# Two transformer blocks on one core: a load, two low parts, a window step and a value product in another order, and banks opened one by one

## The reference

```python
mod = (silu(c) @ w_ada + b_ada)                 # six vectors of 1024: "ada" panels of 512 columns
h = rms_norm(x, norm1_w) * (1 + scale1) + shift1
gq, gk, gv, gz, ga, gb, sq, sk, sv = split(h @ w_in)
beta = sigmoid(gb); g = -exp(a_log) * softplus(ga + dt_bias)     # gates, one row per head
o_g = gated_delta_rule_chunked(l2(gq), l2(gk), gv, g, beta)      # chunks of 64
o_s = sliding_window_attention(rms(sq), rms(sk), sv, sinks)
x = x + gate1 * (concat(o_g, o_s) @ w_out)
x = x + gate2 * ((silu(h2 @ w_gate) * (h2 @ w_up)) @ w_down)
# second block: conformer gate "cu", latent attention over 8 heads, gates "gl"
```

## Time and profile before

| | us |
|---|---|
| median of 3 runs | 1240.29 |
| lowest, highest | 1240.02, 1241.54 |
| the profiled execution | 1240.17 |
| its span, first to last instruction | 1238.1 |
| granted TensorE clock | 1.000 in the mean |
| PE busy | 1211.9 (98%) |
| DVE busy | 707.2 (57%) |
| ACT busy | 505.1 (41%) |
| POOL busy | 107.8 (9%) |
| HBM | 124 MB, 100 GB/s over the span |

### The profile page before, as it was taken

The page is one execution under the profiler, slowest core; times in us unless marked ns, Lnnn a source line. Parts: engine busy times, 40 slices in busy tenths (PEclk is TensorE's granted clock), DMA queues, the critical chain, the costliest instruction groups (busy, mean ns, idle before and its releaser), DMA issues.

```text
span 1238.1 us, 19976 instructions
## 1 busy us (share of the span) xinstructions
PE 1211.9 (98%) x8398; PEld 995.2 (80%) x8398; DVE 707.2 (57%) x1036; ACT 505.1 (41%) x795; POOL 107.8 (9%) x152
## 2 busy tenths in 40 slices
PE   6999999999999999999999999999999999999998
PEld 4788778789888888888888889898876778888886
DVE  5899979645485543323233567768765554433344
ACT  4475543663346222222223353225465663222232
POOL 4000006520020000000000110000012310000000
PEclk9999999999999999999999999999999999999999
DMA  9665711003023552243322342234123025333301
GB/s 339 217 213 193 245 35 38 3 4 105 20 86 101 170 162 77 77 128 102 102 77 64 107 138 77 94 94 86 48 69 81 1 73 140 89 91 105 106 35 68
DMA packets 149928, 125.58 MB, mean 101 GB/s; under 512 B 15952, under 2 KB 133489, under 8 KB 149712
## 3 DMA queue, kind: packets, MB, share of 16 engines
q1 hardware_dynamic: 148416, 121.98, 32.5%
q0 software_dynamic: 1232, 2.07, 0.5%
q10 hardware_dynamic: 192, 0.27, 0.1%
HBM read 122.20 MB, written 2.10 MB: 100 GB/s over the span
## 4 chain that ended last, share of the span: by engine, by line
PE 87%; DVE 8%; ACT 2%; issue 1%; DMA 1%; DVEq 0%; POOL 0%; ACTq 0%
PE bank L614 50%; PE bank L921 6%; PE bank L721 4%; PE bank L1397 4%; PE bank L1367 4%; PE bank L1431 4%; PE bank L754 2%; DVE post L2235 2%; PE bank L1286 2%; PE bank L1113 1%; DVE wlo L2201 1%; DVE arena L2353 1%; PE bank L672 1%; PE bank L1322 1%; PE bank L1339 1%
## 5 line engine op out<-in xcount | busy, mean ns | idle before, releaser
L614 PE MATMUL bank<-hsplit,whi 128*128 128x512 f32 (+1 forms) x1840 | 540.5, 378 | 4.1 <-DVE wlo L2201 4.1
L614 PEld LDWEIGHTS bank<-hsplit,whi 128*128 128x128 f32 x1840 | 335.2, 188 | 72.2 <-issue 7.8
L614 PE MATMUL bank<-hsplit,wlo 128*128 128x512 f32 (+1 forms) x920 | 346.0, 376 | 0.0
L2201 DVE TENSOR_TENSOR wlo<-ring,whi 128x2048 fp32r<-128x2048 f32 (+4 forms) x100 | 200.4, 2005 | 178.3 <-ACT whi L1636 178.0
L1636 ACT ACTIVATE whi<-ring 128x2048 fp32r<-128x2048 f32 (+4 forms) x100 | 168.6, 1686 | 125.5 <-DVE xT L2615 53.3
L614 PEld LDWEIGHTS bank<-hsplit,wlo 128*128 128x128 f32 x920 | 172.9, 188 | 32.4
L614 PE MATMUL bank<-a_split,whi 128*128 128x512 f32 x340 | 104.6, 389 | 0.0
L614 PEld LDWEIGHTS bank<-a_split,whi 128*128 128x128 f32 x340 | 63.8, 188 | 13.3
L614 PE MATMUL bank<-a_split,wlo 128*128 128x512 f32 x170 | 66.1, 389 | 0.0
L1579 POOL TENSOR_TENSOR acc<-acc,tb 128x512 f32<-128x512 f32 x12 | 17.8, 1479 | 423.1 <-ACT tb L1904 423.1
L1640 ACT ACTIVATE a_split<-tb 128x512 fp32r<-128x512 f32 x22 | 13.8, 632 | 88.0 <-DVE tb L2665 87.9
(11 more groups left out here) (491 smaller groups left out, 1803.8 us busy)
## 6 DMA issues: line engine op xcount, KB each, us to landing
ring<-in_w_in_dram SPq DMA_DIRECT2D x22, 1024.0 KB, 5.3
ring<-in_w_in_dram SPq DMA_DIRECT2D x34, 512.0 KB, 5.2
ring<-in_w_ada_dram SPq DMA_DIRECT2D x16, 1024.0 KB, 5.2
ring<-in_w_gate_dram SPq DMA_DIRECT2D x11, 1024.0 KB, 5.4
ring<-in_w_up_dram SPq DMA_DIRECT2D x11, 1024.0 KB, 5.3
ring<-in_w_down_dram SPq DMA_DIRECT2D x8, 768.0 KB, 4.8
ring<-in_w_down_dram SPq DMA_DIRECT2D x8, 640.0 KB, 4.4
hscratch<-in_w_ada_dram SPq DMA_DIRECT2D x4, 1024.0 KB, 14.9
```

The source lines that it names most:

```text
L614: last = mm(o[0:m, 0:n], w[:, k, c0:c0 + m], rhs(s, k), start=k + i == 0, stop=k == kn - 1 and i == 2)
L2201: split_lo = splitter(dve, None, lambda lo, src, hi: tt(lo, src, hi, ALU.subtract))
```

## The change

Eight edits, all of order:

- the first half of the eighth ada panel is now followed by sq0, the second half by sq1; ada 9 comes behind as before
- on DVE, `ada_sum(8)` is called in halves, with the `split_lo` that writes sq0's low part between them
- the `split_lo` of gz0 moves from behind `row_parts(1, ...)` to ahead of the wait for `egb`, that is ahead of the 8-row reciprocal
- in the first gz tile `gate_cols` moves from behind k step 5 to behind k step 7
- of the four window steps beside the `p2` gathers on DVE the last one moves ahead of its gather
- the `split_lo` of out3 moves from behind `raw_rest` of m = 3 to just behind `residual` of m = 3
- `first_tiles` opens each tile's bank just before the tile's first matmul
- `ml_values(29)` moves from the end of the attention's loop to behind k step 1 of the first late gl tile, ahead of `ml_turn(30)`

```diff
+        def ada_half_panel(i, h):
+            panel(f"ada{i}{h}", 4, 512, [(0, 512, w_cols(w_ada, 512 * i, 512, 4 * h, 4))], split=False)
+
         def ada_panel(i):
             for h in range(2):
-                panel(f"ada{i}{h}", 4, 512, [(0, 512, w_cols(w_ada, 512 * i, 512, 4 * h, 4))], split=False)
+                ada_half_panel(i, h)
...
         cols_panel("sv", w_in, 2704, 128)
         ada_panel(7)
-        ada_panel(8)
         for i in range(2):
+            ada_half_panel(8, i)
             cols_panel(f"sq{i}", w_in, 2064 + 256 * i)
         ada_panel(9)
...
             def first_tiles(name, chunk_ready, parts, order=range(KD), between={}):
-                outs = [open_tile(pe, *part[0]) for part in parts]
+                outs = []
                 pe.wait_ge(*done("w_lo", name))
                 hi, lo = split_of(name)
                 for at, k in enumerate(order):
                     pe.wait_ge(*chunk_ready(k))
-                    for o, (key, c0, n, rhs) in zip(outs, parts):
+                    for x, (key, c0, n, rhs) in enumerate(parts):
+                        if at == 0:
+                            outs.append(open_tile(pe, *key))
+                        o = outs[x]
...
-            amid_gz = [{1: [(ada, 9)], 3: [(query_lengths, 3)], 5: [(gate_cols,)], 7: [(gate_rows, 0)]},
+            amid_gz = [{1: [(ada, 9)], 3: [(query_lengths, 3)], 7: [(gate_cols,), (gate_rows, 0)]},
                        {3: [(gate_rows, 1)]}, {1: [(gate_rows, 2)], 7: [(gate_rows, 3)]}, {}]
...
-                if u >= 2 and u % 2:
+                if u >= 2 and u % 2 and u < len(MLU) - 1:
                     ml_values(u - 2)
-            amid_gl = {1: [(ml_turn, len(MLU) - 2)], 4: [(ml_turn, len(MLU) - 1)], 7: [(ml_values, len(MLU) - 1)]}
+            amid_gl = {1: [(ml_values, len(MLU) - 3), (ml_turn, len(MLU) - 2)], 4: [(ml_turn, len(MLU) - 1)], 7: [(ml_values, len(MLU) - 1)]}
...
             ada_mod(6)
-            ada_sum(8)
+            ada_sum(8, 0)
             split_lo()
+            ada_sum(8, 1)
...
             link(row_parts(0, grow, HD, HD + 32, 0))
+            split_lo()
             dve.wait_ge(*done("act_vectors", "egb"))
             link(ts(gate_tmp[0][32:40, :], gate_tmp[0][32:40, :], 1.0, None, ALU.add))
             link(v.reciprocal(gate_tmp[0][32:40, :], gate_tmp[0][32:40, :]))
             link(v.tensor_copy(grow[64:72, :], gate_tmp[0][32:40, :]))
             link(tt(glog[32:40, :], gate_tmp[0][32:40, :], grow[32:40, :], ALU.mult))
             link(row_parts(1, glog, 32, 0, 32))
-            split_lo()
...
             for j in range(NJ):
+                if j == NJ - 1:
+                    window(3 * NJ + 1 + j)
                 dve.wait_ge(*copied("p1", j))
                 gather("p2", j)
-                window(3 * NJ + 1 + j)
+                if j < NJ - 1:
+                    window(3 * NJ + 1 + j)
...
             for m in range(KD):
                 residual(("mo", m), m, 16)
-                if m == 0:
+                if m in (0, 3):
                     split_lo()
...
                 raw_rest("2", m, modA2[:, m:m + 1])
-                if m == 3:
-                    split_lo()
```

## The result

The changed kernel takes **1234.26 us** in the median of six runs (1232.18 to 1234.98), and the kernel before, run beside it, 1241.59 (1240.02 to 1242.36): a ratio of 0.9941, 95% interval 0.9931 to 0.9951. Forecast were 1232.7; the forecast alone spans 1231.8 to 1234, and down to its first two rivals it reaches 1236.4. The measured median lies 0.3 above the first of these ends and inside the second. The profiled execution took 1234.98 us for a span of 1233.2, so it lies above the median; why is the main finding of this study.

A forecast was written before the change was run, and what follows sets the result against it. TensorE (PE) was taken as the bound, busy 1211.9 of 1238.1 us, so only its idle time could be won. Six gains summed to 7.6 us: 1240.17 - 7.6 + 0.12 = 1232.7 us, range 1231.8 to 1234, to 1236.4 with rivals 1 and 2.

The forecast's parts named there:

- sq0, 2.2: First sq0 matmul: earlier load and low part between the `ada_sum(8)` halves start it at about 130.6; gain 2.2 us.
- gz0, 1.4: First gz0 matmul: low part written ahead of the 8-row reciprocal, so PE no longer waits; gain 1.4 us, lower bound 0.9.
- rival 1: DVE becomes the bound between 133 and 168 us, both first gains lost at `gate_cols`: 1236.3 us; chance 0.12.
- Window: Window step ahead of the last gather: POOL's product comes earlier and PE starts at 255.45; gain 0.95 us.
- out3: out3's low part behind `residual` 3 ends at 347.2, PE wants it at 349.0; gain 0.85 us, not under 0.6.
- By starts, not by shown ends: Stalls counted from matmul starts rather than estimated ends: sum about 7.7 us instead of 7.0.
- Banks: `cu` panel: banks opened singly let matmuls begin in two free banks during ACT's copies; gain 1.1 us, 0.3 to 1.2.
- values: `ml_values(29)`: two k steps of gl now lie between turn 29 and its values; gain 1.1 us, lower bound 0.8.
- rival 2: The small gains don't come (single waits cost as much as the common one, POOL hinders): 1235.3 us; chance 0.08.
- It adds and removes no instruction; all is order: Premise for the whole change: the edits only reorder existing work, and its parts are then priced one by one.
- Margin 0.3 us: At `gate_cols` behind k = 7: the scan it needs ends at 164.4, PE gets there at 164.8.
- if PE's busy time grew by what its idle time lost: Sign that the prediction is wrong; PE's busy time was expected to stay at 1212 us.

The follow-up runs named there:

- e7: Kernel before with only the new load order (no halves of `ada_sum(8)`), the window step and the single banks: 1241.20 us, ratio 1.0002.
- e8: Kernel before with `ada_sum(8)` halves (old load order), gz0's low part earlier (`gate_cols` left at k = 5), out3 and value products: 1239.20 us, ratio 0.9985.
- e2: Changed kernel with `gate_cols` put back behind k step 5, the other seven edits kept: 1233.81 us, ratio 0.9943.
- e1: Changed kernel run again with nothing edited: 1234.04 us, ratio 0.9946.
- e3: Changed kernel with `gate_rows(0)` moved on behind k step 1 of the second gz tile: 1232.10 us, ratio 0.9929.
- e5: Changed kernel, small groups still side by side, bank waits removed by moving DVE's ada 8 and 9 sums and ACT's gz 0 copy earlier: 1232.43 us, ratio 0.9930.
- e9: Kernel before run again unchanged, for a profile: 1241.48 us at a clock of 0.997.
- e6: Version of e3 with ScalarE's Ln and its table load moved behind the copy and square of the first sq tile: 1231.89 us, ratio 0.9926.
- e10: Version of e6 with the old load order of sq0 and `ada_sum(8)` in one piece: 1236.93 us, ratio 0.9965.
- e4: Kernel before with one edit alone, `gate_cols` moved behind k step 7, right ahead of `gate_rows(0)`: 1242.49 us, ratio 1.0014.
- run 24: Not a label but a count: 24 of 45 runs of the unchanged kernel before show a clock of 0.997 or less, median 1241.9 us.

## Why the prediction was right, and where it was not

The forecast of 1232.7 lies 1.6 us below the measured median, which is inside its range down to the rivals; its six terms come to 7.6 us where the trace shows 7.85. The six gains came as the mechanism had it. Step by step, with the steps of the table:

- **sq0, 2.2:** 2.17. The matmul follows the L818 pair at 130.00 without a bracket. Both edits are needed (e7, e8).
- **gz0, 1.4:** 1.31, no bracket. DVE did not become the bound (rival 1): the scan ends at 163.95 and PE asks at 164.72. e2 shows the 0.94 us that it would have waited at the old place.
- **Window, out3:** 0.96 and 0.84 for 0.95 and 0.85. The prediction said that the moved low part would meet POOL's sum of m = 3. In the changed kernel that sum is 2.61 us long at 344.22, beside a low part at 343.40 of the usual 2.28, and PE isn't held up. By the Trainium skill, page "SBUF — State Buffer", section "Who interferes with whom", whoever comes first blocks the other; the low part came first and kept its time, which agrees.
- **Banks, values:** 1.28 and 1.29 for 1.1 each; separate waits between matmuls cost nothing that shows (rival 2 is out).
- **By starts, not by shown ends:** the idle brackets add up to 7.04, the shifts to 7.85. The Trainium skill, page "Perfetto Trace Analysis", section "Tensor Engine Instruction (MATMUL, LD_WEIGHTS)", says that ends are estimated; the rows side with it, and the sum by starts was the better one.

Two steps failed. The first is "**It adds and removes no instruction; all is order**", as carried out for `gate_cols`: I asked only whether its input, the scan, would be there ("Margin 0.3 us"), and not which banks it and `gate_rows(0)` take when nothing stands between them. The program hands banks out in turn, so five in a row reach into banks whose readers stand behind gz1's low part on DVE and behind two copies on ACT. The wait is short (by starts 0.40 us in the first profile, 0.93 in e1), but 8 of 11 runs show a fall, which cost 3.0 us in the profile. That the bank waits decide is what e3 and e5 say together: with them gone 9 of 10 runs are at 0.999 or more, whether the small groups stand apart or not. How they bring the clock down is not shown; in the first profile only the first wait lies before the fall.

The second is that DVE's and PE's earlier work was followed, and **ACT's was not**: with sq0 2.2 us earlier, the Ln and its table load (ended at 138.45) hold the copy and the square that `query_lengths` waits for. This cost 0.50 us in the first profile, where sq1's load came late, 0.13 in e3 and nothing in e1: a margin of zero that the sum had no line for, more than a loss of a fixed size.

That the result is near all the same is in part luck, and a matter of the base. The kernel before has a fall in about half of its runs, at the very wait that the change removes (e9). Runs without a fall compare, by their medians, as 1240.38 before and 1232.30 after, 8.1 us less; runs with one as 1241.93 and 1234.26, 7.7 less. The prediction's sign for its own failure, "if PE's busy time grew by what its idle time lost", did show, in part: 2.3 us of it. It was named without a mechanism or a chance, and it should have been a rival: a step whose matmuls are all small, beside two banks that come late, with a price of 3 us.

What stays open: why the longer bank wait in e1 was followed by no fall and the shorter one of the first profile was, why some falls last 6.8 us and others 3.4, and what sets the share of runs that have one. In e2 a wait of 0.94 us ahead of the small matmuls gave one fall in five. The share was not measured against the length of a wait alone.

The version that beats both kernels is e6: 1231.89 us, 2.4 us below the changed kernel and 9.3 below the 1241.20 of the kernel before beside it.

## What to carry to other kernels

When small steps are put side by side, count the banks (or buffers) that they take in turn and look up who frees each: an input that is in time is only half of the question. Where PE is busy nearly all the time, price a wait in its middle at its length plus the chance of a slow clock behind it, and read the granted clock of every run before a median is compared with another. Behind a wait that is removed, follow each engine that now gets its work earlier, also the one that was not late before.

## What the runs showed of the hardware

- PE's granted clock fell from 2.4 to 1.2 GHz in the middle of a kernel that is 98% busy, and came back while PE was working: after 6.8 us in the changed kernel, e9 and e10, after 3.4 us in e4, e7 and e8. (Behind PE's last matmul every kept profile has a half clock too, which costs nothing.) In each of the six PE had stood idle at most 1.7 us before or still did: 2.20 us (e9), 2.15 (e10), 3.43 (e7), 1.18 (e8), 0.64 (e4), and in the changed kernel one matmul came 0.40 us late behind 64 small ones.
- A wait doesn't decide it: 0.54 us in e1, 0.94 in e2 and 2.14 in the first profile of the kernel before were followed by no fall.
- It is not the same from run to run. By the mean clock of a run 24 of 45 runs of the kernel before have it, 8 of 11 of the changed kernel, 10 of 11 of e4, 4 of 5 of e10, all 20 of e7 and e8, none of e3 and e6.
- One fall of 6.8 us costs 3.0 to 3.2 us where PE is the bound behind it (the changed kernel, e9, e10), one of 3.4 us costs 1.5 to 1.6 (e4, e7, e8). In e9 a later wait of PE gave 1.4 of it back.
- 67 matmuls of 40 rows in a row, some 2.8 us, did not bring the clock down in the profile of e5.
